# Decode values of two samples on one set of partitions, with a two-column moving operand

## What is computed

```
for each group g of (window, dilation) = (128,1), (512,4), (2048,16):
  for each sample b, head h:
    keys m = 0..127: rows m*dilation of the cached window, and the new token
    p  = softmax over all of them                    # merged over the groups by their denominators
    att[b, h] += sum over m of p[g, b, h, m] * V[g, b, m, h, :]  + p_new * v_new
```

## Time and profile before

| | us |
|---|---|
| median of 3 runs | 2255.03 (2254.84 to 2255.72) |
| profiled execution | 2255.15 |
| its span | 2253.3 |
| PE busy in the span | 2239.6 |
| DVE busy | 1384.2 |
| ACT busy | 993.1 |
| POOL busy | 474.7 |

### The profile page before, as it was taken

The page is one execution under the profiler, slowest core; times in us unless marked ns, Lnnn a source line. Parts: engine busy times, 40 slices in busy tenths (PEclk is TensorE's granted clock), DMA queues, the critical chain, the costliest instruction groups (busy, mean ns, idle before and its releaser), DMA issues.

```text
span 2253.3 us, 48669 instructions
## 1 busy us (share of the span) xinstructions
PE 2239.6 (99%) x19164; PEld 2225.4 (99%) x19164; DVE 1384.2 (61%) x1439; ACT 993.1 (44%) x1245; POOL 474.7 (21%) x530
## 2 busy tenths in 40 slices
PE   8999999999999999999999999999999999999999
PEld 8999999999999999999999999999999999999999
DVE  6556456765455758886659867665554555544555
ACT  5554334433344543444455665444343344333442
POOL 3487013320000205763306630100000000000000
PEclk9999999999999999999999999999999999999999
DMA  7878778887776678658958875577877778657764
GB/s 216 270 240 270 251 234 272 264 253 238 234 245 204 221 263 261 204 186 295 306 179 288 266 230 179 178 229 250 254 231 229 239 241 259 213 178 235 242 195 142
DMA packets 440669, 528.55 MB, mean 235 GB/s; under 512 B 41352, under 2 KB 421312, under 8 KB 436720
## 3 DMA queue, kind: packets, MB, share of 16 engines
q1 hardware_dynamic: 425504, 508.70, 71.6%
q0 software_dynamic: 3248, 11.62, 1.5%
q10 hardware_dynamic: 11808, 6.70, 1.0%
HBM read 507.80 MB, written 106.09 MB: 272 GB/s over the span
## 4 chain that ended last, share of the span: by engine, by line
PE 91%; DVE 5%; DMA 2%; issue 1%; ACT 1%; ACTq 0%; DVEq 0%; SPq 0%
PE pa L1417 29%; PE pa L1419 29%; PE pa L1418 29%; DVE w_lo L993 2%; DVE head_sd L1174 1%; DMA raw<-in_ffn_w_down 1%; DMA raw<-in_ffn_w_gate 1%; ACT w_hi L607 1%; DVE up_v L1178 0%; PE pb L1674 0%; PE pb L1579 0%; DVE xg_lo L1011 0%; DMA x_rows<-in_x_sample 0%; PE pb L1680 0%; PE pb L1477 0%
## 5 line engine op out<-in xcount | busy, mean ns | idle before, releaser
L993 DVE TENSOR_TENSOR w_lo<-raw,w_hi 128x1024 fp32r<-128x1024 f32 x735 | 941.2, 1293 | 631.2 <-ACT w_hi L607 626.9
L1417 PE MATMUL pa<-xg_hi,w_hi 128*128 128x264 f32 x3968 | 1135.6, 286 | 1.8 <-DVE w_lo L993 1.8
L1418 PE MATMUL pa<-xg_lo,w_hi 128*128 128x264 f32 x3968 | 1127.8, 284 | 0.0
L1419 PE MATMUL pa<-xg_hi,w_lo 128*128 128x264 f32 x3968 | 1126.3, 284 | 0.0
L607 ACT ACTIVATE w_hi<-raw 128x1024 fp32r<-128x1024 f32 x735 | 767.9, 1055 | 748.8 <-PE pa L1419 685.1
L1417 PEld LDWEIGHTS pa<-xg_hi,w_hi 128*128 128x128 f32 x3968 | 747.2, 188 | 4.9 <-issue 1.5
L1418 PEld LDWEIGHTS pa<-xg_lo,w_hi 128*128 128x128 f32 x3968 | 745.8, 188 | 0.6
L1419 PEld LDWEIGHTS pa<-xg_hi,w_lo 128*128 128x128 f32 x3968 | 746.1, 188 | 0.0
L1417 PE MATMUL pa<-act_hi,w_hi 128*128 128x264 f32 x1632 | 463.7, 284 | 0.4 <-DVE w_lo L993 0.4
L1418 PE MATMUL pa<-act_lo,w_hi 128*128 128x264 f32 x1632 | 463.9, 284 | 0.0
L1419 PE MATMUL pa<-act_hi,w_lo 128*128 128x264 f32 x1632 | 463.1, 284 | 0.0
(11 more groups left out here) (329 smaller groups left out, 1518.1 us busy)
## 6 DMA issues: line engine op xcount, KB each, us to landing
raw<-in_ffn_w_gate SPq DMA_DIRECT2D x172, 512.0 KB, 4.7
raw<-in_ffn_w_up SPq DMA_DIRECT2D x172, 512.0 KB, 5.1
out_kv_s<-in_cache_kv_w SPq DMA_DIRECT2D x165, 512.0 KB
raw<-in_ffn_w_down SPq DMA_DIRECT2D x160, 512.0 KB, 4.4
raw<-in_w_in SPq DMA_DIRECT2D x152, 512.0 KB, 5.2
raw<-in_w_out SPq DMA_DIRECT2D x32, 512.0 KB, 4.4
tab<-ssm_tab SPq DMA_DIRECT2D x8, 1152.0 KB, 9.3
raw<-in_w_ssm_branch SPq DMA_DIRECT2D x16, 512.0 KB, 4.2
```

Source lines behind the costliest of these rows:

```text
L993: dve.tensor_tensor(w_lo[:, slot], raw[:, slot], w_hi[:, slot].bitcast(f32), ALU.subtract).then_inc(lo_ready, 1)
L1417: pe.matmul(out, wh, hi, start=first, stop=False)
L1418: pe.matmul(out, wh, lo, start=False, stop=False)
L1419: return pe.matmul(out, wl, hi, start=False, stop=last)
```

## The change

Two samples share the partitions: 64 partitions hold sample 2i, 64 hold sample 2i + 1, and each partition holds two keys, `q` = 0 and 1, as two rows of 512. There are three tiles `vu`, one a group, of 128 x 2 x 512, loaded by two DMAs of 64 partitions each. `pt_dec` is stored in the same arrangement (four copies instead of one). ACT scales a tile with 8 activations. POOL adds the two keys of each tile and then the groups, five adds a pair of samples. PE sums with four matmuls a pair, behind slab 5 only; the moving operand `sample_of` has two columns, ones on the partitions of one sample and zeros on the others. `add_values` runs once a pair.

The order on the engines: SP loads group 0 of the next pair behind slab 2, group 1 behind 3, group 2 behind 5, each after the step that frees the tile. ACT scales group 1 behind slab 0, group 2 behind slab 2, and group 0 of the next pair behind slab 6; in the first iteration the three stand behind slabs 0, 2 and 3. POOL adds group 0 ahead of the first half's recurrence, groups 1 and 1 + 0 between `z_in` and the wait for the scans, and group 2 and 2 + 1 ahead of the second half's.

```diff
+    sample_of = small[:, 4:6]
...
-    vu = [tile(f"vu{k}", [P, NSLOT * HD], f32, RV + 2048 * k) for k in range(6)]
+    vu = [tile(f"vu{g}", [P, 2, NSLOT * HD], f32, RV + 4096 * g) for g in range(NG)]
...
-    pt_dec = tile("pt_dec", [P, NG, NS * NSLOT])
+    pt_dec = tile("pt_dec", [P, 2, NG, NS * NSLOT // 2])
...
+            def load_values(i, g):
+
+                src = caches[g].rearrange("b t (q p r) h d -> b t q p r (h d)", q=2, r=GROUPS[g][1])
+                for half in range(2):
+                    at = slice(64 * half, 64 * half + 64)
+                    sync.dma_start(vu[g][at], src[bass.ds(2 * i + half, 1), 1, :, :, 0, :].rearrange("o q p c -> (o p) q c")).then_inc(vu_loaded[g], 16)
...
+                        for g in range(NG):
+                            load_values(i, g)
+                    if not below(i, 1):
+                        if j == 2:
+                            sync.wait_ge(v_step, 4 * i - 1)
+                            load_values(i, 0)
+                        if j == 3:
+                            sync.wait_ge(v_sum_ready, i)
+                            load_values(i, 1)
+                        if j == 5:
+                            sync.wait_ge(pv_done, i)
+                            load_values(i, 2)
...
+            def scale_values(i, g):
+
+                act.wait_ge(vu_loaded[g], 32 * i + 32)
+                if below(i, 1) and g == 0:
+                    act.wait_ge(dec_ready, 1)
+                for q in range(2):
+                    for hh in range(NSLOT):
+                        v = vu[g][:, q, hh * HD:(hh + 1) * HD]
+                        ins = act.activation(v, v, ACT.Copy, scale=pt_dec[:, q, g, bass.ds(NSLOT * i + hh, 1)])
+                ins.then_inc(vs_ready, 1)
...
-                    if j in (0, 3):
-                        h = j // 3
-                        k = 2 * i + h
-                        act.wait_ge(vu_loaded[h], 48 * i + 48)
-                        if below(i, 1) and h == 0:
-                            act.wait_ge(dec_ready, 1)
-                        for g in range(NG):
-                            for hh in range(NSLOT):
-                                v = vu[3 * h + g][:, hh * HD:(hh + 1) * HD]
-                                ins = act.activation(v, v, ACT.Copy, scale=pt_dec[:, g, bass.ds(NSLOT * k + hh, 1)])
-                        ins.then_inc(vs_ready, 1)
+                    last = isinstance(i, int) and i == ph.iters - 1
+                    if below(i, 1):
+                        if j in (0, 2, 3):
+                            scale_values(i, max(j - 1, 0))
+                    elif j in (0, 2):
+                        scale_values(i, 1 + j // 2)
+                    if j == 6 and not last:
+                        scale_values(i + 1, 0)
...
-                    dve.tensor_copy(pt_dec[:].rearrange("p a b -> p (a b)"), pb[:, 3, 0:96])
+                    weights = pb[:, 3, 0:96].rearrange("p (g i s h) -> p g i s h", g=NG, s=2, h=NSLOT)
+                    for sample in range(2):
+                        for q in range(2):
+                            to, frm = slice(64 * sample, 64 * sample + 64), slice(64 * q, 64 * q + 64)
+                            dve.tensor_copy(pt_dec[to, q].rearrange("p g (i h) -> p g i h", h=NSLOT), weights[frm, :, :, sample])
...
-                dve.tensor_tensor(att_v[:, :, bass.ds(NT + k, 1)], pb[:, 0, PV:PV + NSLOT, None],
-                                  att_new[:, 0, bass.ds(NSLOT * k, NSLOT), None], ALU.add).then_inc(pv_read, 1)
+                dve.tensor_tensor(att_v[:, :, bass.ds(NT + 2 * k, 2)], pb[:, 0, PV:PV + 2 * NSLOT].rearrange("p (h s) -> p h s", s=2),
+                                  att_new[:, 0, bass.ds(2 * NSLOT * k, 2 * NSLOT)].rearrange("p (s h) -> p h s", s=2),
+                                  ALU.add).then_inc(pv_read, 1)
...
+            for half in range(2):
+                dve.memset(sample_of[64 * half:64 * half + 64, half:half + 1], 1.0)
+                dve.memset(sample_of[64 * half:64 * half + 64, 1 - half:2 - half], 0.0)
...
-                        pe.wait_ge(v_sum_ready, k + 1)
-                        if below(i, 1) and h == 0:
-                            pe.wait_ge(att_read, NSLOT)
-                        pe.wait_ge(sv_ready, k + 1)
+                    if j == 5:
+                        pe.wait_ge(v_sum_ready, i + 1)
+                        pe.wait_ge(sv_ready, 2 * i + 2)
                         for hh in range(NSLOT):
-                            ins = pe.matmul(pb[:, 0, PV + hh:PV + hh + 1], vu[3 * h][:, hh * HD:(hh + 1) * HD], ones[:, 0:1],
+                            ins = pe.matmul(pb[:, 0, PV + 2 * hh:PV + 2 * hh + 2], vu[2][:, 0, hh * HD:(hh + 1) * HD], sample_of,
...
+            def add(to, other):
+
+                return pool.tensor_tensor(to, to, other, ALU.add)
+
             def gates_b(i):
                 for h in range(2):
                     k = 2 * i + h
-                    pool.wait_ge(vs_ready, k + 1)
-                    pool.tensor_tensor(vu[3 * h][:], vu[3 * h][:], vu[3 * h + 1][:], ALU.add).then_inc(v_step, 1)
-                    pool.wait_ge(v_step, k + 1)
-                    pool.tensor_tensor(vu[3 * h][:], vu[3 * h][:], vu[3 * h + 2][:], ALU.add).then_inc(v_sum_ready, 1)
+                    if h == 0:
+                        pool.wait_ge(vs_ready, 3 * i + 1)
+                        add(vu[0][:, 0], vu[0][:, 1]).then_inc(v_step, 1)
+                    else:
+                        pool.wait_ge(vs_ready, 3 * i + 3)
+                        add(vu[2][:, 0], vu[2][:, 1]).then_inc(v_step, 1)
+                        pool.wait_ge(v_step, 4 * i + 4)
+                        add(vu[2][:, 0], vu[1][:, 0]).then_inc(v_sum_ready, 1)
...
                     pool.tensor_tensor(z_in[:, 0], p_tmp[:, 0], p_tmp[:, 1], ALU.add).then_inc(zr_ready, 1)
+                    if h == 0:
+                        pool.wait_ge(vs_ready, 3 * i + 2)
+                        add(vu[1][:, 0], vu[1][:, 1]).then_inc(v_step, 1)
+                        pool.wait_ge(v_step, 4 * i + 2)
+                        add(vu[1][:, 0], vu[0][:, 0]).then_inc(v_step, 1)
```

More of the change, by code:

```diff
@@ L210, in build_layer @@
     vec = tile("vec", [P, NV])
-    small = tile("small", [P, 4])
+    small = tile("small", [P, 6])
     eps_t, halfpi_t = small[:, 0:1], small[:, 1:2]
+    sample_of = small[:, 4:6]
     RX = region(CH)
@@ L332, in build_layer @@
     qb_loaded = [nc.alloc_semaphore(f"qb_loaded{k}") for k in range(2)]
-    vu_loaded = [nc.alloc_semaphore(f"vu_loaded{k}") for k in range(2)]
+    vu_loaded = [nc.alloc_semaphore(f"vu_loaded{g}") for g in range(NG)]
     prod_ready, sc_ready, kq_ready, ds_done, dmax_ready, dexp_ready, dec_step, diag_ready, dt_done, dec_ready = sems(
@@ new lines, in gates_b @@
+                    if below(i, 1) and j == 1:
+                        sync.wait_ge(prod_ready, len(UNITS))
+                        sync.wait_ge(qk_ready, 2 * NH)
+                        sync.wait_ge(rows_stored, ROWS_STORED)
+                        for kv in range(2):
+                            for g in range(NG):
+                                dst = new_caches[g][:, kv, GROUPS[g][0] - 1].rearrange("b h d -> b (h d)")
+                                sync.dma_start(dst, kv_dram[kv, g]).then_inc(stored, 16)
+                                n_stored[0] += 16
+                        for g in range(NG):
+                            load_values(i, g)
@@ L849, in gates_b @@
                     if isinstance(i, int) and i == ph.iters - 1 and j == 6:
-                        act.wait_ge(pv_read, NS)
+                        act.wait_ge(pv_read, NS // 2)
                         act.activation(att_hi[:, :, NT:T], att_v[:, :, NT:T], ACT.Copy).then_inc(att_hi_ready, 1)
@@ L1255, in gates_b @@
                     if last:
-                        add_values(NS - 1)
+                        add_values(i)
                     if j in (2, 5):
@@ L1270, in gates_b @@
                                           d_tmp[:, 1].rearrange("p (t c) -> p t c", t=4), ALU.add).then_inc(xi_ready, 1)
-                    if j in (2, 5) and not last:
-                        add_values(2 * i + j // 4)
+                    if j == 5 and not last:
+                        add_values(i)
                     if below(i, 1) and j == 0:
@@ L1696, in gates_b @@
                             pe.wait_ge(u4_loaded, 16 * 48)
-                        else:
-                            pe.wait_ge(pv_read, k)
+                        elif h == 0:
+                            pe.wait_ge(pv_read, i)
                         for m in range(4):
@@ L2036, in _ @@
                     pool.dma_start(ys_v[row:row + 16], u4[at:at + 16, 2 * (jj // 2) + g::4, 0:NS]).then_inc(yl_loaded, 16)
-            pool.wait_ge(pv_done, NS)
+            pool.wait_ge(pv_done, NS // 2)
             step = Chain(pool, xnew_step)
```

3 lines of the change are left out of this document (removed).

## The result

The changed kernel took 2267.41 us (median of 5, 2266.39 to 2268.24) against 2255.03: a ratio of 1.0055, 95% interval 1.0043 to 1.0066, slower by 12.4 us where 6.4 were forecast. Its profiled execution took 2266.64 us, span 2264.8, 11.5 above the span before.

The account below looks back on a forecast made before the run. PE bounds the stage by share, with the ACT, DVE and POOL recurrence at nearly zero slack; delays of 1.49 + 1.73 + 1.47 + 1.73 = 6.4 us on 2255.0 gave 2261.4, range 2255.5 to 2267.

Parts of the forecast that it names:

- turn-taking: First-half recurrence: a two-input SBUF operation of DVE or POOL runs only when the other's has ended; 1.15 us per add.
- tight place: POOL's gap between z_in and its wait for the scan, idle 1.21 us before; the two adds put 2.30 there.
- S + 11.47: Forecast first state product, S being the first L1417 matmul behind the input products; S + 9.74 before in iteration 1.
- Rival A: POOL's middle adds hide beside DVE's recurrence: 2254.5 to 2257 us, chance 0.17.
- removed sums: PE's slab 2 value sums, 0.81 us an iteration, become idle time and gain 0, since xi and xr end last.
- L993 at 2 us instead of 1.19: Sign of a right forecast: DVE's L993 between the scans and xs lengthens in the first halves.
- 2.54 of new PE idle time: First half of iteration 1: PE's new wait before its first state product at 1227.03, 1.73 us later than before.
- rival C: New 2.5 us PE idle stretches lower the granted clock: 9.6 us on top, about 2271, chance 0.10.
- Loads ... the same bytes ... 0, at worst 1 us an iteration: SP issues six loads of 64 partitions for six of 128; price 0, at worst 1 us an iteration.
- rival D: A late load or SP wait delays the scaling or slabs behind slab 6: 2264 to 2268, chance 0.10.
- ACT's part at slab 6: Scaling for the next pair waits for a recent load; price 0, up to 1 us in three iterations if cover fails.
- the memsets and the copies of pt_dec: Four memsets ahead of PE's first work, at most 0.2 us; three more DVE copies, before idle time: both 0.

Follow-up runs that it names:

- e9: Changed kernel with samples on alternating partitions, weights arranged to match, and 20 filler transposes on PE ahead of the first half's output products: 2260.90 us.
- e8: Kernel before with two extra 512-column scratch adds on POOL between z_in and the wait for the scans, first halves only: 2264.51 us.
- e12: Kernel before with four POOL memsets of 512 to 528 columns between z_in and the wait for the scans, first halves only: 2255.69 us.
- e1: Changed kernel with the two middle adds moved ahead of the first half's recurrence in iterations 1 to 3: 2262.72 us.
- e3: Changed kernel with the two middle adds left out altogether: 2260.96 us.
- e10: Changed kernel with alternating-partition loads, weights arranged to match, middle adds ahead of the recurrence in iterations 1 to 3, behind it in iteration 0: 2255.79 us.
- e4: Changed kernel with groups 0 and 1 loading only a quarter of each row from iteration 1 on: 2266.01 us.
- e5: Changed kernel with the two samples of a pair on alternating partitions instead of two blocks of 64: 2267.47 us.
- e11: Changed kernel, own loads and weights, with middle adds ahead of the recurrence in iterations 1 to 3, behind it in iteration 0: 2262.15 us.
- e7: Kernel before with each 128-partition value load issued as two loads of 64 partitions: 2255.34 us.
- e2: Changed kernel with 20 filler transposes on PE ahead of the wait for xr and xi in each first half: 2266.68 us.

## Why the prediction was wrong

**The turn-taking was right, and so was its price.** The two adds take turns with DVE in the tight place. e9, with the turn-taking alone, is 6.0 us above before where the sum said 6.4 (5.5 of it in the stretches); its stretches of 11.15 to 11.31 stand against a forecast S + 11.47. The sums of the sequence hold to 0.03 us. e8 makes the same stretches in the kernel before, e12 shows that it is the adds and not POOL's being busy, and e1, e3 and e10 take the stretches back to 9.1 to 9.5 wherever no slab is late. Rival A (the adds hide) is out. The removed sums are worth nothing while the recurrence ends last, as said; with the adds out of the way PE does reach its products at S + 9.2, and e10 has 2.05 us less in its first halves (37.41 against 39.46) and loses the same 2.05 in iteration 0's second half. The sign "L993 at 2 us instead of 1.19" came in two iterations of four; in the others the adds were ahead of both scans, which bore the wait in its place.

**The step that failed first: the clock, at nothing in the sum.** "2.54 of new PE idle time" stood in the forecast itself, and its effect on the clock was set aside as rival C with a chance of 0.10; the argument against it was the full clock of a profile without such a wait. In the changed kernel the half clock followed two of the four stretches, those of 3.15 and 3.41 us without PE work, at 3.0 us each (rival C had 2.4 each, in four places). It doesn't need the late slabs: e4 and e5 have none in iterations 1 to 3, PE waits 2.1 to 2.3 us there, near the forecast's 2.54, and two spells follow in each; their times stay at 2266.01 and 2267.47. With PE's waits filled it is gone, and e9 against e5 is 6.6 us. The length alone does not decide: of e4's four waits of 2.2 to 2.4 us (11.15 to 11.31 less 8.93) two are followed by a spell, and e8's one spell stands behind a wait of 1.6 (11.32 less 9.74), while three waits of 1.5 to 1.8 before it have none. But no kernel whose PE had work throughout shows one. What decides between two waits of one length no run shows.

**The second step: "Loads ... the same bytes ... 0, at worst 1 us an iteration".** The bytes are the same, but a packet into a block of 64 partitions took 147 ns instead of 101. The slabs behind these loads came late, and ACT splits one of them just ahead of sv. Iterations 1 and 3 are 0.8 and 1.2 us over e9's for it, 2.0 us, about the bound by themselves. Their larger effect is again through PE's wait: in e11, where the adds are out of the way, the late slab of iteration 3 alone makes PE wait and a long spell follows, and e11 is 6.4 us above e10. That is rival D's mechanism (0.10), entered through the packets' duration rather than a wait of SP's. The time lies in D's 2264 to 2268, but by luck: D's 1 to 2 us an iteration were 2.0 in all, and the clock made the rest.

The Trainium skill ("DMA: Bandwidth & Descriptors", Rules for kernel authors) says of two transfers to disjoint halves of the partitions that they share the same engines, and to use one of 128 instead. I did not weigh it. By it the loads gain nothing from the split, and e7 agrees (0.55 us over its group's before, with an interval of 0.9994 to 1.0012 that holds 1). That a packet becomes dearer these rules do not say.

**The sum as it should have been.** In the profiled execution the terms are 5.7 for the turn-taking (forecast 6.4), 2.0 for the slabs and 6.0 for the clock, less 2.2 at the stage's ends (1.2 of them the `att_lo` wait that the last spell used up): 11.5. The terms don't stand apart, since a wait of PE from either cause can bring a spell: e5 (slabs mended) and e2 (waits filled, a slab still late) stay at 2267.47 and 2266.68, and only e9, with both, comes down to the turn-taking's price. The range stopped at 2267 because the clock and the late loads were taken as alternatives to the forecast, each with its own chance, while the waits that lower the clock are the forecast's own.

Smaller steps: the two-column value sum takes 0.81 us as the one-column one did (L1737 above). ACT's part at slab 6, the memsets and the copies of pt_dec left no mark that can be told from the 2.8 us by which the stage's begin varies from the changed kernel to e1 to e4.

## What to carry to other kernels

Before a step is put into an engine's gap next to a recurrence of another engine, look at whether both have two inputs in SBUF, as the adds, the multiplies, the scans and the subtraction here: the gap is then not free, though a memset in it is. What an operation with one input costs there no run shows. When a forecast contains a new wait of TensorE, price the half clock behind it in the same sum, and see whether filler work costs less than the wait. "The same bytes" is no price for a load: compare the duration of its packets, and what is queued behind it.

## What was not expected of the hardware

- Loads into 64 adjoining partitions, two rows each: 147 ns a packet of 2048 bytes; on alternating partitions 106, in 128-partition loads 101, in 64-partition loads of one row each 117.
- GpSimd's memsets (0.53 us for 528 columns) leave VectorE's scans at 1.12 and 0.66 us; its adds make them 1.67 and 1.71.
- 2.35 us of transposes without use in each of four places made the kernel 6.6 us faster (e9 against e5), with PE's wait there filled.
- Waits of PE as short as 1.6 us (e8) and 2.3 us (e4) were followed by a spell at half clock in a stage otherwise at full clock, others of the same length by none.
